# First mixer of a two-layer encoder on one core: input blocks 1 to 4 in three passes over split operands

## What is computed

```python
def even_mixer(h, w_in, ...):                     # h = rmsnorm(x), 512 x 1024
    q, k, v, glu = split(h @ w_in, ...)           # 512 columns each, glu 1024
    o = diff_attention(q1, q2, k1, k2, v, lam, rel_bias)   # 4 heads, 128-query blocks, block-causal
    o = o * rsqrt(mean(o * o) + EPS) * subln_g * (1.0 - lam_init)
    c = c_val * sigmoid(c_gate)
    c = causal_depthwise_conv(c, conv_w, conv_b)  # 31 taps over positions, 512 channels
    c = silu(layernorm(c, conv_ln_g, conv_ln_b))
    return concatenate([o, c]) @ w_out
...
x = x + even_mixer(...); x = x + peer(...)        # layer 0
x = x + gla_mixer(...);  x = x + peer(...)        # layer 1
```

## Time and profile before

| | us |
|---|---|
| median of 3 runs | 2789.14 (2783.98 to 2794.88) |
| profiled execution | 2784.39, its span 2782.6 |
| TensorE busy | 2745.1 (99%) |
| VectorE busy | 2355.9 (85%) |
| ScalarE busy | 1080.1 (39%) |
| GpSimd busy | 759.7 (27%) |
| mean granted TensorE clock | 0.999 |
| plain fp32 units of the projection, L1579 | 224 records, 96.3 |

### The profile page before, as it was taken

One profiled execution on the slowest core, in us unless ns is written; L12 is line 12 of the kernel. 1 busy time (PEld: TensorE's weight loads), 2 busy tenths in 40 slices (PEclk: granted clock), 3 DMA queues, 4 the chain that ended last, 5 costly groups with the idle time before them and its releaser, 6 DMA issues.

```text
span 2782.6 us, 40826 instructions
## 1 busy us (share of the span) xinstructions
PE 2745.1 (99%) x15202; PEld 1611.3 (58%) x15298; DVE 2355.9 (85%) x4000; ACT 1080.1 (39%) x1426; POOL 759.7 (27%) x519
## 2 busy tenths in 40 slices
PE   9999999999999999999999999999999999999999
PEld 5455666666666444444467776666666664444444
DVE  6955899997998899999753578999889988999996
ACT  2163333334555333333343443333345543333333
POOL 0000222222323454545100002222222334545450
PEclk9999999999999999999999999999999999999999
DMA  4213677768999999999612246767689999999993
GB/s 162 91 51 140 251 264 267 273 212 308 353 354 349 384 390 396 400 400 390 264 35 91 80 185 243 286 259 265 249 305 346 363 358 382 396 394 404 391 398 149
DMA packets 216248, 784.48 MB, mean 282 GB/s; under 512 B 14740, under 2 KB 101272, under 8 KB 196152
## 3 DMA queue, kind: packets, MB, share of 16 engines
q1 hardware_dynamic: 50352, 421.08, 39.4%
q0 software_dynamic: 73728, 268.47, 25.1%
q10 hardware_dynamic: 92040, 93.33, 10.0%
HBM read 686.09 MB, written 96.73 MB: 281 GB/s over the span
## 4 chain that ended last, share of the span: by engine, by line
PE 58%; issue 12%; DVE 11%; PEld 8%; DVEq 4%; ACT 3%; DMA 2%; PEldq 1%; POOL 0%; ACTq 0%; SPq 0%
PE ps L2013 12%; PE ps L2015 12%; PE ps L2014 12%; PEld ps L2090 8%; DVE x_res L1287 3%; DVE arena L1247 3%; PE ps L2090 2%; PE ps L1978 2%; DVE arena L1051 2%; ACT arena L786 2%; PE ps L1970 2%; PE ps L1986 2%; PE ps L1667 2%; PE ps L2071 2%; PE ps L2072 2%
## 5 line engine op out<-in xcount | busy, mean ns | idle before, releaser
L2090 PE MATMUL ps<-arena 128*128 128x512 bf16 x4488 | 985.3, 379 | 9.5 <-DVE arena L1441 4.3
L536 POOL DMA_INDIRECT arena<-in_ur,arena x256 | 361.4, 1412 | 1502.5 <-DVE arena L1278 884.5
L2090 PEld LDWEIGHTS ps<-arena 128*128 128x128 bf16 x4584 | 448.2, 98 | 545.7 <-issue 4.4
L2013 PE MATMUL ps<-xnh,arena 128*128 128x384 bf16 x2048 | 667.5, 326 | 3.9 <-DVE arena L1239 3.9
L2015 PE MATMUL ps<-xnh,arena 128*128 128x384 bf16 x2048 | 667.5, 326 | 0.0
L2014 PE MATMUL ps<-xnl,arena 128*128 128x384 bf16 x2048 | 667.5, 326 | 0.0
L1247 DVE TENSOR_TENSOR arena<-arena 128x2048 bf16<-128x2048 f32 x250 | 571.3, 2290 | 72.0 <-ACT arena L786 66.0
L786 ACT ACTIVATE arena<-arena 128x1024 bf16<-128x1024 f32 x512 | 524.4, 1048 | 75.3 <-PE ps L2090 34.5
L536 POOL DMA_INDIRECT arena<-in_v,arena x256 | 396.6, 1549 | 405.6 <-DVE x_res L1287 343.8
L1287 DVE SCALAR_TENSOR_TENSOR x_res<-arena,x_res 128x1024 f32<-128x1024 f32 x256 | 328.6, 1283 | 20.7 <-issue 0.4
L820 ACT ACTIVATE arena<-ps 128x384 f32<-128x384 f32 x256 | 125.5, 490 | 515.9 <-PE ps L2015 515.8
(11 more groups left out here) (262 smaller groups left out, 2787.1 us busy)
## 6 DMA issues: line engine op xcount, KB each, us to landing
arena<-in_v SPq DMA_DIRECT2D x64, 2048.0 KB, 10.2
arena<-in_u SPq DMA_DIRECT2D x62, 2048.0 KB, 10.3
h_scratch<-arena ACTq DMA_DIRECT2D x60, 768.0 KB
arena<-h_scratch SPq DMA_DIRECT2D x60, 768.0 KB, 8.5
arena<-gate_scratch SPq DMA_DIRECT2D x64, 640.0 KB, 6.9
arena<-in_wmix SPq DMA_DIRECT2D x14, 2048.0 KB, 7.9
...
```

Source lines behind the costliest of these rows:

```text
L536: pool.indirect_dma_start(ring[n % NBUF], None, ur_d[L] if g < P else vr_d[L], at).then_inc(gat_in[n % NBUF], 16)
L2013: pe.matmul(ps[:, j % 2, 0:TD], uh, xnh[:, kd], start=kd == 0, stop=False)
L2090: last = pe.matmul(ps[:, 2 + 2 * tt + dh], c, v[:, TPG * s + q, dh * 512:(dh + 1) * 512], start=start and c is ch and v is hi, stop=stop a ...
```

## The change

Blocks 1 to 4 (the second half of the gated channels, q, k, v) are multiplied in three passes over split operands instead of plain fp32; block 0 stays plain. For that:

- **ScalarE** makes rounded copies of the tokens (t_high; six parts into `x_lo[0]`, two into `t_hi6` and the new buffer `t_hi7`) ahead of its first evacuation, and of the weights of a block (`weights_hi0`, four copies of 128x1024, m_high) behind evacuations of the blocks before: block 1 behind unit 1, block 2 behind unit 5, blocks 3 and 4 behind the second unit of q and of k.
- **VectorE** makes the token rests in place of xnT (`token_rest`, t_rest) behind the first 16 taps, once the four units of block 0 are done.
- **GpSimd** makes the weight rests in place of the weights (`weights_lo0`, m_low), four subtractions of 128x1024 per block, each behind its rounded copy.
- **TensorE** has 24 matmuls a unit instead of eight plain ones: rounded by rounded, rounded weights by token rests, weight rests by rounded tokens; in the first two units of block 1 the token rests come last. A values unit is spread over attention units in parts of 12, 12; 12, 12; and four of 6.
- **Convolution**: the last 15 taps of tiles 2 and 3 (30 instructions) move from ahead of attention into units 0 to 3. The norm moves too: sums from ahead of unit 0 to unit 4, the matmul with ones to unit 5, the mean to unit 6 (read from an evacuated copy instead of PSUM), squares to unit 7, root from unit 3 to 9, reciprocal from 3 to 10, products from 5 to 10, silu from 6 to 11. The last values unit is evacuated in unit 12 instead of 11.
- `relb8` moves into the arena, where its space is free at that time, and the unit count ahead of block 6's load is 22 instead of 21, since the matmul of the mean is now a unit.

```diff
@@ -216,6 +216,14 @@
...
+        t_lo = x_hi
+        t_hi6 = rounded("t_hi6", 39168, T)
+        t_hi7 = ctx.enter_context(nc.sbuf_tensor("t_hi7", [P, T], F32R))
+        m_whi = [rounded(f"m_whi{s}", 14336 + 4096 * s, KD, 512) for s in range(2)]
+        def t_hi(kd):
+            return x_lo[0][:, kd] if kd < 6 else (t_hi6, t_hi7)[kd - 6][:]
@@ -384,7 +396,7 @@
...
-        U0 = 21
+        U0 = 22
@@ -526,6 +538,19 @@
...
+            def weights_lo0(b):
+                for kd in range(0, KD, 2):
+                    at = slice(kd, kd + 2)
+                    pool.wait_ge(m_high, KD * (b - 1) + kd + 2)
+                    pool.tensor_tensor(w_lo[b % 2][:, at], wblk[b % 2][:, at], m_whi[b % 2][:, at].bitcast(F32),
+                                       ALU.subtract).then_inc(m_low, 2)
+            weights_lo0(1)
+            weights_lo0(2)
+            weights_lo0(3)
+            weights_lo0(4)
@@ -604,13 +629,31 @@
...
                 act.activation(lame[:], ps[:, 3, 256:258], ACT.Exp).then_inc(setup_ev, 1)
-                for n in range(2):
-                    for c in range(2):
-                        unit_out(m_up[:, 2 * n + c, TAPS - 1:])
-                        unit_out(m_sig[:, 2 * n + c], ACT.Sigmoid)
-                for dst in (m_qT, m_kT):
+                act.wait_ge(xt_high, TT)
+                act.drain()
+                for kd in range(0, 6, 2):
+                    act.activation(x_lo[0][:, kd:kd + 2], xnT[:, kd:kd + 2], ACT.Copy).then_inc(t_high, 2)
+                for kd in range(6, KD):
+                    act.activation(t_hi(kd), xnT[:, kd], ACT.Copy).then_inc(t_high, 1)
+                def weights_hi0(b):
+                    act.wait_ge(w_in[b % 2], 16 * (b // 2 + 1))
+                    if b >= 3:
+                        act.wait_ge(p_done, 4 * (b - 1))
+                    for kd in range(0, KD, 2):
+                        at = slice(kd, kd + 2)
+                        act.activation(m_whi[b % 2][:, at], wblk[b % 2][:, at], ACT.Copy).then_inc(m_high, 2)
+                for ct in range(CT):
+                    unit_out(m_up[:, ct, TAPS - 1:])
+                    unit_out(m_sig[:, ct], ACT.Sigmoid)
+                    if ct % 2 == 0:
+                        weights_hi0(1 + ct // 2)
+                for n, dst in enumerate((m_qT, m_kT)):
...
                         unit_out(dst[:, c])
+                        if c == 1:
+                            weights_hi0(3 + n)
@@ -640,26 +683,30 @@
...
                     if u == 1:
+                        unit_out(m_v[:, 0])
+                    if u == 3:
+                        unit_out(m_v[:, 1])
+                    if u == 5:
+                        unit_out(m_v[:, 2])
+                    if u == 6:
+                        unit_out(m_sig[:, 3], scale=-1.0 / (CT * P))
+                        act.drain().then_inc(st_done, 1)
+                    if u == 7:
...
                             act.activation(m_sq[:, ct], m_y[:, ct], ACT.Square).then_inc(sq_ready, 1)
-                        unit_out(m_v[:, 0])
-                    if u == 3:
+                    if u == 9:
...
                         act.drain().then_inc(p_free, 1)
-                    if u == 4:
-                        unit_out(m_v[:, 1])
-                    if u == 6:
+                    if u == 11:
...
                                            scale=cols[:, C_LNG + ct:C_LNG + ct + 1]).then_inc(conv_out, 1)
-                    if u == 7:
-                        unit_out(m_v[:, 2])
-                    if u == 11:
+                    if u == 12:
@@ -1050,22 +1097,36 @@
...
+                def token_rest():
+                    dve.wait_ge(p_done, 4)
+                    dve.wait_ge(t_high, KD)
+                    for kd in range(0, 6, 2):
+                        dve.tensor_tensor(t_lo[:, kd:kd + 2], xnT[:, kd:kd + 2], x_lo[0][:, kd:kd + 2].bitcast(F32),
+                                          ALU.subtract).then_inc(t_rest, 2)
+                    for kd in range(6, KD):
+                        dve.tensor_tensor(t_lo[:, kd], xnT[:, kd], t_hi(kd).bitcast(F32), ALU.subtract).then_inc(t_rest, 1)
                 tapped = [0] * CT
-                for channels, count in (((0,), 16), ((0, 1), 15), ((1, 2), 8), ((1, 3), 8), ((2, 3), 23)):
+                def taps(channels, count):
...
                         for ct in channels:
-                            last = tap(ct, tapped[ct])
+                            tap(ct, tapped[ct])
...
+                for channels, count in (((0,), 16), ((0, 1), 15), ((1, 2), 8), ((1, 3), 8), ((2, 3), 8)):
+                    taps(channels, count)
+                    if channels == (0,):
+                        token_rest()
...
                         dve.scalar_tensor_tensor(nlam[:], lame[:, 1:2], -LAM_INIT, lame[:, 0:1], ALU.add, ALU.subtract)
-                assert tapped == [TAPS] * CT
@@ -1099,23 +1160,27 @@
...
                 logits(1)
-                dve.tensor_tensor(m_sig[:, 0], m_y[:, 0], m_y[:, 1], ALU.add)
-                dve.tensor_tensor(m_sig[:, 1], m_y[:, 2], m_y[:, 3], ALU.add)
-                dve.drain()
-                dve.tensor_tensor(m_sig[:, 0], m_sig[:, 0], m_sig[:, 1], ALU.add).then_inc(conv_done, 1)
...
                     combine(u)
-                    if u == 0:
+                    if u == 6:
...
                         for ct in range(CT):
-                            dve.scalar_tensor_tensor(m_y[:, ct], ps[:, 7], -1.0 / (CT * P), m_y[:, ct],
-                                                     ALU.mult, ALU.add).then_inc(yc_ready, 1)
+                            dve.tensor_tensor(m_y[:, ct], m_y[:, ct], m_sig[:, 3], ALU.add).then_inc(yc_ready, 1)
...
                         logits(u + 2)
-                    if u == 1:
+                    if u < 4:
+                        taps((2, 3), 3 if u == 3 else 4)
+                    if u == 4:
+                        assert tapped == [TAPS] * CT
+                        dve.drain()
+                        dve.tensor_tensor(m_sig[:, 2], m_y[:, 0], m_y[:, 1], ALU.add)
+                        dve.tensor_tensor(m_sig[:, 3], m_y[:, 2], m_y[:, 3], ALU.add)
+                        dve.drain()
+                        dve.tensor_tensor(m_sig[:, 2], m_sig[:, 2], m_sig[:, 3], ALU.add).then_inc(conv_done, 1)
+                    if u == 7:
@@ -1123,11 +1188,11 @@
...
                         values_out(u - 2)
-                    if u == 3:
+                    if u == 10:
...
                         dve.drain()
-                    if u == 5:
+                    if u == 10:
@@ -1713,11 +1778,37 @@
...
                     by_columns(0, c)
-                for c in (0, 2, 1, 3):
-                    by_columns(1, c)
-                for b in range(2, 4):
-                    for c in range(4):
-                        by_columns(b, c)
+                def high_high(bank, b, c):
+                    pe.wait_ge(m_high, KD * b)
+                    pe.wait_ge(t_high, KD)
+                    for kd in range(KD):
+                        pe.matmul(bank, m_whi[b % 2][:, kd, c * P:(c + 1) * P], t_hi(kd), start=kd == 0, stop=False)
+                def high_rest(bank, b, c, stop):
+                    pe.wait_ge(t_rest, KD)
+                    for kd in range(KD):
+                        last = pe.matmul(bank, m_whi[b % 2][:, kd, c * P:(c + 1) * P], t_lo[:, kd], start=False,
+                                         stop=stop and kd == KD - 1)
+                    return last
+                def low_high(bank, b, c, stop):
+                    pe.wait_ge(m_low, KD * b)
+                    for kd in range(KD):
+                        last = pe.matmul(bank, w_lo[b % 2][:, kd, c * P:(c + 1) * P], t_hi(kd), start=False,
+                                         stop=stop and kd == KD - 1)
+                    return last
+                banks = unit_bank(), unit_bank()
+                for bank, c in zip(banks, (0, 2)):
+                    high_high(bank, 1, c)
+                    low_high(bank, 1, c, False)
+                for bank, c in zip(banks, (0, 2)):
+                    high_rest(bank, 1, c, True).then_inc(p_done, 1)
+                for b, c in [(1, 1), (1, 3)] + [(b, c) for b in (2, 3) for c in range(4)]:
+                    bank = unit_bank()
+                    high_high(bank, b, c)
+                    high_rest(bank, b, c, False)
+                    low_high(bank, b, c, True).then_inc(p_done, 1)
@@ -1746,12 +1837,10 @@
...
                     pe.wait_ge(pt_out, u + 1)
-                    if u == 0:
-                        pe.wait_ge(yc_ready, CT)
-                    else:
+                    if u:
...
                     if h == 0:
-                        pe.wait_ge(p_free, (17, 19, 20, 21)[i])
+                        pe.wait_ge(p_free, (17, 18, 19, 22)[i])
@@ -1759,9 +1848,14 @@
...
                     at = slice(tt * P, (tt + 1) * P)
-                    for kd in range(first, first + count):
```

(47 more changed lines are left out.)

12 lines of the change are left out of this document (8 added, 4 removed).

## The result

| | median of runs, us | runs, us | profiled execution, us | its span, us |
|---|---|---|---|---|
| before | 2787.83 | 2783.98 to 2794.88 | 2784.4 | 2782.6 |
| after | 2825.46 | 2814.81 to 2830.29 | 2830.29 | 2828.3 |

The changed kernel takes 1.0129 times as long (95% interval 1.0096 to 1.0161): 37.6 us more between the medians. The forecast was 2818, inside a range of 2784 to 2834.

The account below looks back on a forecast made before the run. TensorE and VectorE, ending together ahead of attention, were taken to bound the kernel. First read of logits +12, attention +19.9 and TensorE's clock +2 made +34 on 2784.4 us: 2818, range 2784 to 2834.

Parts of the forecast that it names:

- What bounds the kernel: Ahead of attention TensorE and VectorE end together, so both need relief; each microsecond the output projection's start moves counts whole.
- TensorE's part: Projections: split units of 5.44 us instead of 6.87 save 17.2 us, and 6.6 us among attention units; together 23.8 us.
- ScalarE's part: Rounded copies of tokens and weights, ahead of and behind evacuations in the projections, were to cost 0.
- VectorE's part ahead of attention: Thirty taps leave (-22.3 us), token rests come (+5.0); first read of logits at 108.7 us without anything else.
- GpSimd's part, the deciding price: Sixteen weight subtractions beside VectorE's taps hold VectorE 1.8 us each: +29 us (23 to 50), first read at 138.
- The attention stage: With taps and norm moved among its units, attention takes 89.4 us instead of 69.5: +19.9.
- TensorE's clock: The clock falls in TensorE's 22 us wait for logits, slowing the units after it: +2 us.
- the dearer rivals: In attention the clock stays low to unit 7 or 11: +7 or +13, 2823 to 2829 us; clock or hold dearer, chance 0.08.
- Sum: First read +12, attention +19.9, clock +2: +34 us on the profiled execution's 2784.4, giving 2818 us.
- No port conflict: GpSimd's subtractions don't hold VectorE's taps: -17.3 + 19.9 = +2.6, clock 0 to 2, 2787 us; chance 0.22.
- The smaller hold: Each GpSimd subtraction costs VectorE 1.45 us: +28, 2812 us; within the 0.60 chance for 1.45 to 2.1 us each.
- Faster: No conflict, and the deferred taps fill VectorE's waits in attention, stage at 72 us: -15, 2770 us; chance 0.10.

Follow-up runs that it names:

- reorder_only: Changed kernel with input projections back to plain fp32, no weight rests or GpSimd work; only the new placing of taps and norm kept: 2809.44 us, ratio 1.0068.
- pool_writes: Changed kernel with GpSimd's sixteen subtractions replaced by memsets of the same tiles, which read nothing: 2797.89 us (one run).
- psum_taps: Changed kernel with the running sum of the taps ahead of attention in PSUM instead of SBUF, GpSimd's subtractions kept: 2798.7 us, ratio 1.0032.
- pool_one_input: Changed kernel with GpSimd's sixteen subtractions replaced by copies with one SBUF input, so the function isn't computed: 2804.97 us (one run).
- warm_gap: Changed kernel with 90 products of zeros on TensorE ahead of the logits of unit 2 and 8 in each of units 1 and 2: 2822.34 us, ratio 1.0125.
- old_order: Changed kernel with all 124 taps ahead of attention and the norm back at units 0 to 6; split products and GpSimd's subtractions kept: 2825.05 us, ratio 1.0127.

## Why the prediction was right, point by point

**What bounds the kernel.** Right. reorder_only shows one half (TensorE alone left as it was: first read at 125.6 on its shifted scale) and pool_writes and psum_taps the other (both relieved: about 110). That nothing past the output projection changes held only roughly: the output start moved 35.2 us, the profiled span 45.7. The 10.5 us between lie behind it, in stages that the change doesn't touch; over the executions profiled here the stretch from output start to end takes 2587 to 2598 us, with before's at the low end (2587.1) and after's at the high one (2597.6). By the medians (+37.6) most of that is scatter.

**TensorE's part.** Right: unit 5.45 us (start to start), forecast 5.44. It was to wait some 4.5 us for the tokens' rests and end at 113; it waited 5.25, and the sixteen products behind that wait took 5.48 us instead of 3.6, with the granted clock at 0.72 from 56 to 62 us. It ended at 116.3, hidden as forecast.

**ScalarE's part.** Right: 0. Four copies ahead of each group of subtractions, and no wait of VectorE or TensorE on them; TensorE's one wait for ScalarE from 28 to 116 us is 0.73 us, for an evacuation.

**VectorE's part ahead of attention.** 108.7 without conflict; psum_taps has 110.54 and pool_writes 110.19, of which the last 1.26 us are TensorE's. Right to 2 us.

**GpSimd's part, the deciding price.** The mechanism is shown by psum_taps. Its size was a little low: 1.8 us for one subtraction, measured (140.93 - 108.7)/16 = 2.01 by the forecast's own base, 1.94 from first tap to first read against psum_taps ((109.69 - 78.64)/16), and 2.03 from first to last tap against pool_writes ((109.77 - 77.27)/16). First read at 140.9, forecast 138. The one row of 128x256, read as an exclusive hold and scaled by four, came within 0.2 us. That scaling was in part luck: it takes the length of an operation to grow in proportion to its size, but four times that row's 0.84 is 3.4 us, and the subtraction takes 2.41 in psum_taps and 2.84 beside the taps. The forecast's upper end, 3.4 us sixteen times, is 54 and not 50, and the stated range of the time ends below either. The Trainium skill's figure ("GPSIMD Engine Reference", section Elementwise — side-by-side cycle accounting: 4497 ns for 2048 fp32 elements, an estimate of 2.2 us each) was 0.2 too high as the price, and as the operation's own duration it is too low: 2410 ns undisturbed. The rule in "SBUF — State Buffer" of the Trainium skill, section Who interferes with whom, agrees with psum_taps, in which the accumulator in PSUM ends the hold, and with pool_one_input, in which a copy that reads SBUF still holds the taps; the price, 0.68 us for a copy and 2.0 for a subtraction, only the runs give.

**The attention stage.** Forecast 89.4, and 91.4 with the clock; measured 89.7. By quarters, first read to turn 4, 8, 12 and the output start, beside the same quarters of warm_gap, in which the gap ahead of the stage is filled:

| quarter | forecast, without the clock | after | warm_gap |
|---|---|---|---|
| units 0 to 3 | 32.6 | 31.3 | 31.2 |
| units 4 to 7 | 16.6 | 18.0 | 16.6 |
| units 8 to 11 | 22.5 | 23.4 | 22.7 |
| units 12 to 15 | 15.8 | 17.0 | 17.0 |
| sum | 87.5 | 89.7 | 87.5 |

The layout was 1.3 us too long in the first quarter and 1.2 too short in the last, where the trace of before already had 17.1; that its sum is warm_gap's is luck, since these misses cancel. (The parts that the forecast lists for units 0 to 3 come to 31.6 us, or 32.2 with 0.6 for each values_out, and not to its 32.6.) I had taken from it only the difference to the old layout (67.6) and added that to the trace's 69.5, which carried the old layout's miss of 1.9 us over to the new order; that is the term's error. The chain between combines 10 and 12 took 12.7 us for 12.0. reorder_only (90.4), old_order (69.3) and psum_taps (88.3) give the stage's +20 to the placing alone.

**TensorE's clock.** +2 forecast; 2.2 measured for the gap. The size agrees, the place does not: the forecast saw the cost in units 0 to 3, and it lies between turns 4 and 9. The granted clock was 0.57 on average in the gap, 0.84 and 0.85 in attention, and it stayed under 1.00 up to turn 12 (0.83, 0.79, 0.80 by quarters). So the condition of the dearer rivals, a low clock to unit 7 or 11, came true in part, and their prices (+7, +13) did not: with them the stage would have taken 94.5 to 100.5 us by the layout's 87.5, and it took 89.7.

**Sum.** The term of the first read was 2.9 us low (+12 forecast, +14.9), attention with its clock 1.7 high (+21.9 forecast, +20.2): output start +35.2 for +34. The time came out 7.5 us above 2818, of which 1.2 are this; 3.4 are the base, since I had summed from the profiled execution (2784.4), that much below the median; the rest lies behind the output start (+37.6 between the medians for +35.2) and in rounding, and is within the scatter of the runs.

**Rivals.** No port conflict is out by the changed kernel's own rows (the longest tap is 2902 ns). The smaller hold (1.45) is out: 1.94 to 2.03. *Faster*, by taps that fill VectorE's waits, is out by reorder_only, and by psum_taps, where the hold is gone and the stage still takes 88.3 us.
